# Two decoder layers on one core: GpSimd's shift products of the second pair behind a border, with and without a wait for the inverse root

## The chip, the cores and the metric
The kernel runs on one core of a Trainium2 chip, with TensorE (PE), VectorE (DVE), ScalarE (ACT), GpSimd (POOL) and SyncE (SP), which issues the weight loads. The metric is device time in microseconds of one execution, as the median of several runs.

## The reference, cut to what matters
Two layers of a decoder, 512 tokens, width 1024, float32. Each layer has three sub-layers, each with its own norm, and each norm is modulated by a shift and a scale worked out from a conditioning vector:

```python
h = modulate(rmsnorm(x, norm_ffn1[l]), sh1, sc1)
x = x + 0.5 * g1[:, None, :] * swiglu(h, ffn1_w_up[l], ffn1_w_down[l])
h = modulate(rmsnorm(x, norm_mix[l]), sh2, sc2)
x = x + g2[:, None, :] * hybrid_mixer(h, ...)
h = modulate(rmsnorm(x, norm_ffn2[l]), sh3, sc3)
x = x + 0.5 * g3[:, None, :] * swiglu(h, ffn2_w_up[l], ffn2_w_down[l])
```

with `rmsnorm(x) = x * rsqrt(mean(x*x) + eps) * gain` and `modulate(h) = h * (1 + scale) + shift`. `swiglu` multiplies by a 1024 x 5632 matrix, takes silu(gate) * up, and multiplies by a 2816 x 1024 matrix. So a product of weights with a normalised input is W(x * gain * (1 + scale)) * r + W shift, where r, the inverse root, is one number for each token, and W shift is one number for each output column.

## The kernel before, in words
Activations lie transposed: 128 features of a tile on the partitions, the 512 tokens along the row, 8 tiles `XV[:, k, :]`. Every product is done in three matmuls (`product`, L1598 to L1602): weights and activations are each split in a high part that is rounded (`hi`) and the rest (`lo`), and hi*hi, hi*lo and lo*hi are summed in a PSUM bank. A **unit** is one 128-column tile of weights against all 512 tokens, 8 times 3 matmuls (11 times 3 in the down projection). Units come in **pairs** `b`, unit `s=0` and `s=1`, and so do the buffers `raw[s]`, `Whi[s]`, `Wlo[s]`. SP loads `raw[s]` (L365), ACT makes `Whi` (L568), DVE makes `Wlo` (L943), PE consumes both (L1600 to L1602). ACT's split of a unit waits until PE is through with the unit before it in the same buffer.

The **borders** are the places where one sub-layer ends and the norm of the next begins. PE would be idle there until the sum of squares, its inverse root and the normalised tiles are made. So the first two pairs behind a border are computed from x * gain without the root (`scaled_hi` L614, `scaled_lo` L1010), and afterwards multiplied by the root and given the shift's contribution W shift. In front of the feed-forward borders this is done for the first pair (p=0) and the second pair (p=1); the third pair reads properly normalised tiles. The kernel has three such borders with a second pair: before ffn2 of layer 0, before ffn1 of layer 1, and before ffn2 of layer 1. The two borders before the mixer have a first pair only.

What W shift takes: GpSimd's `shift_products` (L473) multiplies the raw weights of a unit by the shift (L489, 1024 elements a partition), folds them in two halvings (L494, 512 and then 256 elements a partition) and a last one (L497, 128 elements). That is four instructions for a unit, eight for a pair. PE turns the result into a column (`shift_sums`, L1632) and DVE copies that (L1031). For every pair, SP may load the next weights into `raw[s]` only when GpSimd has read it (`shift_read`). GpSimd also adds the squares (`add_squares`, L471) that ACT makes (L579).

The order at such a border, each engine's queue being in program order:
- GpSimd: the adds of squares; shift products of pair p=0, unit 0, then (in between, or behind it before ffn1) the last add of squares, unit 1; then pair p=1, both units. Before the products of p=1 it waits for `rstd_ready`, which DVE's inverse root raises (L477 to L479).
- PE: unit 0 of the first pair (`first_pair`, L1635). After its tile k=2 it does the sum of squares (`sum_squares`, L1593); in unit 1, after tile k=2 (`SPREAD_AT`), it waits for the inverse root and spreads it over the partitions (`spread_rstd`, L1659). Then the shift sums of p=0, two units of the second pair (into the banks `ps_mid`), then the third pair, tile by tile as `split_lo` says that a normalised tile is there.
- DVE: `rstd_of` (L978), a chain of 12 instructions on 4 numbers a partition, each waiting for the one before: L984 (reads PSUM), L985, L986, then three times L990, L991, L992. Behind it, in `first_pairs` (L1033), come the split of a unit of weights, the first normalised tile (`tile`, L1017, which waits for PE's spread), `lo` (L1025), the copies of shift columns, the gates (L1041, L1047, L1049), with more tiles and weight splits in between, up to `lo(7)`.
- ACT: weight splits (L568), the high parts of normalised tiles (L625), silu of the gate (L641), in `first_pairs` (L633).

The call for the second pair is, before ffn2 and before ffn1 of the next layer:

```python
shift_products(l, "ffn2", pair_no(l, FFN2), 1, mod_done, fold_no(l, MIX_FOLD) + 2)
...
shift_products(l + 1, "ffn1", pair_no(l + 1, 0), 1, mod_done, fold_no(l, NEXT_FOLD) + 2)
```

Of the kernel before, what the change touches and what calls it, by code (L numbers as in the profile page):

```python
# [111 lines left out]
def decoder(nc, x, c, positions, norm_ffn1, norm_mix, norm_ffn2, final_norm, w_ada, b_ada,  # L112
# [5 lines left out]
    with ctx:  # L118
# [3 lines left out]
        def sem(name):  # L122
            return ctx.enter_context(nc.semaphore(name))
# [98 lines left out]
        sq_ready, sq_used, ss_ready, rstd_ready, rb_ready = sem("sq_ready"), sem("sq_used"), sem("ss_ready"), sem("rstd_ready"), sem("rb_ready")  # L222
# [17 lines left out]
        carrier = {"sp": sem("sp_carrier"), "pool": sem("pool_carrier"), "dve": sem("dve_carrier")}  # L240
# [38 lines left out]
        def pair_no(l, off):  # L279
            return l * LAYER_PAIRS + off  # L280
# [8 lines left out]
        def fold_no(l, n):  # L289
            return FOLDS * l + n  # L290
# [5 lines left out]
        NORM_NO = {"ffn1": 0, "mix": 1, "ret": 2, "ffn2": 3}  # L296
# [12 lines left out]
        def shift_no(l, name):  # L309
            return LAYER_SHIFTS * l + SHIFT_NO[name]  # L310
# [25 lines left out]
        def angles(eng, st, col, n, ang, tmp):  # L336

            def op(out, in0, *a):
                st.mark(eng.tensor_scalar(out, in0, *a))
                st.wait()  # L340

            op(ang, pos_f[:, :], K[:, K_COL + col:K_COL + col + 1], None, ALU.mult)
            op(n, ang, 1.0 / TWO_PI, ROUND, ALU.mult, ALU.add)
            op(n, n, ROUND, None, ALU.subtract)
            for part in (C1, C2, C3):
                op(tmp, n, part, None, ALU.mult)
                st.mark(eng.tensor_tensor(ang, ang, tmp, ALU.subtract))
                st.wait()
            return eng.tensor_scalar(ang, ang, float(np.float32(-3.1415925)), float(np.float32(3.1415925)), ALU.max, ALU.min)
# [102 lines left out]
        @block.gpsimd  # L452
        def _(pool):
            st = Steps(pool, pool_step)
            pool.wait_ge(const_in, 16 * 2)
            pool.wait_ge(vec_in, 16 * (5 + DEPTH))
            pool.tensor_copy(pos_f[:, :], pos_i[:, :]).then_inc(pos_done, 1)
            pool.wait_ge(pos_done, 1)
            pool.wait_ge(unit_done, 2 * HALF + 3)
            angle_tmp = pos_i[:, :].bitcast(F)  # L460
            angles(pool, st, 0, cos_r[:, :], sin_r[:, :], angle_tmp).then_inc(ang_done_r, 1)
            pool.wait_ge(ang_done_r, 1)
            angles(pool, st, 2, cos_s[:, :], sin_s[:, :], angle_tmp).then_inc(ang_done_s, 1)

            def add_squares(no, k):

                pool.wait_ge(sq_ready, KT * no + k + 1)
                if k > 1:
                    pool.wait_ge(sq_used, ADDED * no + k - 1)
                pool.sem_inc(carrier["pool"], 1)  # L470
                pool.tensor_tensor(square_sum, square_sum, squares[:, k % 2, :], ALU.add).then_inc(sq_used, 1)  # L471

            def shift_products(l, name, b, p, ready, value, between=lambda: None):  # L473

                pool.wait_ge(ready, value)
                pool.sem_inc(carrier["pool"], 1)
                if p:  # L477
                    pool.wait_ge(rstd_ready, 4 * l + NORM_NO[name] + 1)
                    pool.sem_inc(carrier["pool"], 1)  # L479
                for s in range(2):  # L480
                    if s:
                        between()
                    no, acc = shift_no(l, name) + 2 * p + s, shift_acc[2 * p + s]
                    if not isinstance(no, int) or no > 0:
                        pool.wait_ge(shift_made, no)
                    pool.wait_ge(landed[s], 16 * (b + p + 1))
                    pool.sem_inc(carrier["pool"], 1)
                    shift = mod[:, MOD_COL[name]:MOD_COL[name] + KT].unsqueeze(2).broadcast_to([P, KT, P])
                    pool.tensor_tensor(shift_tmp.rearrange("p (k c) -> p k c", c=P), raw[s][:, 0:UP_UNIT].rearrange("p (k c) -> p k c", c=P),  # L489
                                       shift, ALU.mult).then_inc(shift_read, 1)  # L490
                    pool.wait_ge(shift_read, no + 1)
                    pool.sem_inc(carrier["pool"], 1)
                    for n in (UP_UNIT // 2, UP_UNIT // 4):
                        st.mark(pool.tensor_tensor(shift_tmp[:, 0:n], shift_tmp[:, 0:n], shift_tmp[:, n:2 * n], ALU.add))  # L494
                        st.wait()
                        pool.sem_inc(carrier["pool"], 1)
                    pool.tensor_tensor(acc, shift_tmp[:, 0:P], shift_tmp[:, P:2 * P], ALU.add).then_inc(shift_made, 1)  # L497

            with st.loop(0, DEPTH, LAYER_SHIFTS * 2) as l:
                for k in range(1, ADDED):  # L500
                    add_squares(3 * l + 1, k)
                shift_products(l, "mix", pair_no(l, KV_PAIR), 0, mod_done, fold_no(l, MIX_FOLD) + 2,
                               lambda: add_squares(3 * l + 1, ADDED))

                pool.wait_ge(ss_ready, 3 * l + 2)
                pool.sem_inc(carrier["pool"], 1)
                pool.memset(k_all[:, :, 0:P], 0.0).then_inc(k_zero, 1)
                pool.wait_ge(k_zero, l + 1)
                pool.wait_ge(v_done, 2 * TT * (l + 1))
                pool.wait_ge(sv_done, l + 1)  # L510
                pool.wait_ge(k_done, l + 1)
                pool.sem_inc(carrier["pool"], 1)
                def sum_pairs(i):

                    pool.wait_ge(ysq, 2 * (RH * l + i) + 2)
                    pool.sem_inc(carrier["pool"], 1)
                    pool.tensor_tensor(probs[1][:, 0:T], probs[1][:, 0:T], probs[1][:, T:2 * T], ALU.add).then_inc(ysum, 1)

                for i in range(RH):
                    if i % 2 == 0:  # L520

                        pool.wait_ge(unit_done, 2 * pair_no(l, HEAD0) + 6 * i + 2)
                        pool.sem_inc(carrier["pool"], 1)
                        pool.tensor_copy(k_cur, k_all[:, i // 2, :]).then_inc(key_in, 2)

                    pool.wait_ge(y_ps, RH * l + i + 1)
                    pool.sem_inc(carrier["pool"], 1)
                    if i % 2:
                        pool.tensor_copy(v_cur, V[:, i]).then_inc(head_in, 1)
                    else:  # L530
                        pool.tensor_copy(v_cur, V[:, i])
                        pool.wait_ge(o_ps, 2 * (RH * l + i))
                        pool.sem_inc(carrier["pool"], 1)
                        pool.tensor_copy(sv_cur, sv_all[:, i // 2]).then_inc(head_in, 1)
                    if i:
                        sum_pairs(i - 1)
                sum_pairs(RH - 1)
                for k in range(1, ADDED):
                    add_squares(3 * l + 2, k)
                shift_products(l, "ffn2", pair_no(l, FFN2), 0, mod_done, fold_no(l, MIX_FOLD) + 2,  # L540
                               lambda: add_squares(3 * l + 2, ADDED))
                shift_products(l, "ffn2", pair_no(l, FFN2), 1, mod_done, fold_no(l, MIX_FOLD) + 2)
                for k in range(1, ADDED):
                    add_squares(3 * l + 3, k)
                with pool.If(l < DEPTH - 1):
                    shift_products(l + 1, "ffn1", pair_no(l + 1, 0), 0, mod_done, fold_no(l, NEXT_FOLD) + 2)
                add_squares(3 * l + 3, ADDED)
                with pool.If(l < DEPTH - 1):
                    shift_products(l + 1, "ffn1", pair_no(l + 1, 0), 1, mod_done, fold_no(l, NEXT_FOLD) + 2)
# [1437 lines left out]
```

## Time and profile before
| | us |
|---|---|
| median of 3 runs | 2506.55 (2506.16 to 2508.14) |
| the profiled execution | 2506.7 |
| its span, first to last instruction | 2504.9 |
| PE busy | 2472.0 (99%) |
| DVE busy | 1501.5 (60%) |
| ACT busy | 872.2 (35%) |
| GpSimd busy | 210.3 (8%) |

The profile lists busy time by engine over one execution. Times of rows are microseconds from the start of the span. A row of the timeline has its start, its duration, the engine, the line of the kernel, the operation, what it writes and reads, and in brackets the idle time of the engine before it with what ended it. A duration counts from when the engine took the instruction up, so that a time in which it could not get at its data lies inside the duration.

### The profile page before, as it was taken

To read this page: it belongs to the slowest core of one execution; us is meant where nothing else is said; L and a number is where in the kernel's file an instruction comes from. 1 tells how busy PE (TensorE), PEld (TensorE's weight loads), DVE (VectorE), ACT (ScalarE), POOL (GpSimd) and SP (SyncE) were. 2 spreads that over 40 slices of the span, in tenths; PEclk is the share of its full clock that TensorE was granted. 3 is DMA by queue.
4 is the path that set the end of the run, shared out by engine and by line. 5 is a ranking of instruction groups with operands and counts; after the bars stand their busy time and mean duration, and the time that the engine had idled before them with its cause. 6 is when DMAs were issued, how large, how long until landed. Compare 5 with 4: busy or idle time off the path is not lost.

```text
span 2504.9 us, 35621 instructions
## 1 busy us (share of the span) xinstructions
PE 2472.0 (99%) x11468; PEld 2012.8 (80%) x11468; DVE 1501.5 (60%) x2297; ACT 872.2 (35%) x1326; POOL 210.3 (8%) x151
## 2 busy tenths in 40 slices
PE   7999999999999999999999999999999999999998
PEld 5888888877788878888878888887777888788887
DVE  5677778677643477533467677877775435633332
ACT  3222333555423343222332223345553323331332
POOL 0013002000000040000140000210100002200001
PEclk9999999999999999999999999999999999999999
DMA  6665664222134336433336656532222343333332
GB/s 246 195 188 173 187 181 148 86 66 59 53 92 133 94 91 196 140 101 100 102 97 198 186 174 197 165 116 78 59 59 65 95 134 93 88 106 88 96 105 80
DMA packets 488916, 307.31 MB, mean 123 GB/s; under 512 B 9000, under 2 KB 480376, under 8 KB 488184
## 3 DMA queue, kind: packets, MB, share of 16 engines
q1 hardware_dynamic: 420816, 238.73, 32.2%
q10 hardware_dynamic: 68008, 67.48, 8.5%
q8 instruction: 41, 0.67, 0.1%
q14 instruction: 51, 0.42, 0.1%
HBM read 299.89 MB, written 6.29 MB: 122 GB/s over the span
## 4 chain that ended last, share of the span: by engine, by line
PE 94%; DVE 2%; issue 1%; ACT 1%; DMA 0%; DVEq 0%; SPq 0%; ACTq 0%
PE ps_proj L1600 28%; PE ps_proj L1602 28%; PE ps_proj L1601 28%; PE ps_mid L1870 1%; PE ps_mid L1766 1%; PE ps_o L1787 1%; PE ps_mid L1817 1%; PE ps_mid L1819 1%; PE ps_mid L1818 1%; PE ps_mid L1774 1%; PE ps_mid L1862 1%; DMA sb_scratch<-in_x 0%; DVE sb_scratch L1017 0%; PE ps_small L1593 0%; ACT sb_w_hi L568 0%
## 5 line engine op out<-in xcount | busy, mean ns | idle before, releaser
L1600 PE MATMUL ps_proj<-sb_a_hi,sb_w_hi 128*128 128x512 f32 x1908 | 745.5, 391 | 2.2 <-ACT sb_scratch L681 1.7
L1602 PE MATMUL ps_proj<-sb_a_hi,sb_w_lo 128*128 128x512 f32 x1908 | 742.8, 389 | 0.0
L1601 PE MATMUL ps_proj<-sb_a_lo,sb_w_hi 128*128 128x512 f32 x1908 | 742.8, 389 | 0.0
L568 ACT ACTIVATE sb_w_hi<-sb_raw 128x1024 fp32r<-128x1024 f32 (+1 forms) x388 | 430.9, 1110 | 849.1 <-PE ps_proj L1602 816.2
L943 DVE TENSOR_TENSOR sb_w_lo<-sb_raw,sb_w_hi 128x1024 fp32r<-128x1024 f32 (+1 forms) x388 | 514.1, 1325 | 323.2 <-ACT sb_w_hi L568 315.4
L1600 PE MATMUL ps_proj<-sb_h_hi,sb_w_hi 128*128 128x512 f32 x1212 | 480.1, 396 | 6.0 <-DVE sb_h_lo L1025 3.9
L1602 PE MATMUL ps_proj<-sb_h_hi,sb_w_lo 128*128 128x512 f32 x1212 | 472.4, 390 | 0.0
L1601 PE MATMUL ps_proj<-sb_h_lo,sb_w_hi 128*128 128x512 f32 x1212 | 472.2, 390 | 0.0
L1600 PEld LDWEIGHTS ps_proj<-sb_a_hi,sb_w_hi 128*128 128x128 f32 x1908 | 358.5, 188 | 78.7 <-ACT sb_scratch L681 3.0
L1602 PEld LDWEIGHTS ps_proj<-sb_a_hi,sb_w_lo 128*128 128x128 f32 x1908 | 358.4, 188 | 74.6
L1601 PEld LDWEIGHTS ps_proj<-sb_a_lo,sb_w_hi 128*128 128x128 f32 x1908 | 358.6, 188 | 74.3 <-issue 0.5
L1600 PEld LDWEIGHTS ps_proj<-sb_h_hi,sb_w_hi 128*128 128x128 f32 x1212 | 227.6, 188 | 66.4 <-issue 14.0
L1602 PEld LDWEIGHTS ps_proj<-sb_h_hi,sb_w_lo 128*128 128x128 f32 x1212 | 227.6, 188 | 48.5
L1601 PEld LDWEIGHTS ps_proj<-sb_h_lo,sb_w_hi 128*128 128x128 f32 x1212 | 227.7, 188 | 45.3
L955 DVE SCALAR_TENSOR_TENSOR sb_scratch<-sb_scratch,sb_c_act 128x256 f32<-128x256 f32 x448 | 223.7, 499 | 16.1
L471 POOL TENSOR_TENSOR sb_scratch<-sb_scratch 128x512 f32<-128x512 f32 x36 | 61.3, 1702 | 1567.1 <-ACT sb_scratch L579 1567.1
L1097 DVE SCALAR_TENSOR_TENSOR sb_x_or_values<-ps_proj,sb_half_gate,sb_x_or_values 128x512 f32 (+1 forms) x80 | 60.0, 750 | 198.5 <-PE ps_proj L1602 196.9
L1121 DVE TENSOR_TENSOR sb_scratch<-sb_scratch,ps_proj 128x512 f32<-128x512 f32 x82 | 56.4, 688 | 173.7 <-PE ps_proj L1602 173.5
L681 ACT ACTIVATE sb_scratch<-ps_proj 128x512 f32<-128x512 f32 x82 | 49.0, 598 | 303.8 <-PE ps_proj L1602 303.8
L752 ACT ACTIVATE sb_scratch<-sb_scratch,sb_small 128x256 f32<-128x256 f32 x128 | 63.1, 495 | 0.0
L1010 DVE SCALAR_TENSOR_TENSOR sb_h_lo<-sb_x_or_values,sb_gain,sb_h_hi (+1 forms) x40 | 58.7, 1467 | 5.6 <-ACT sb_h_hi L614 5.0
L1124 DVE TENSOR_TENSOR sb_a_lo<-sb_scratch,sb_a_hi 128x512 f32 (+1 forms) x82 | 56.1, 684 | 0.0
(210 smaller groups left out, 1824.6 us busy)
## 6 DMA issues: line engine op xcount, KB each, us to landing
sb_raw<-in_ffn_w_up SPq DMA_DIRECT2D x176, 512.0 KB, 3.8
sb_scratch<-in_w_ada ACTq DMA_DIRECT2D x128, 512.0 KB, 4.2
sb_raw<-in_w_in SPq DMA_DIRECT2D x100, 512.0 KB, 3.8
sb_raw<-in_ffn_w_down SPq DMA_DIRECT2D x64, 704.0 KB, 4.5
sb_raw<-in_w_branch_swa SPq DMA_DIRECT2D x16, 512.0 KB, 3.6
sb_raw<-in_w_branch_ret SPq DMA_DIRECT2D x16, 512.0 KB, 3.6
sb_raw<-in_w_out SPq DMA_DIRECT2D x16, 512.0 KB, 3.5
sb_scratch<-in_w_ada SPq DMA_DIRECT2D x10, 512.0 KB, 7.4
```

What stands on the lines that cost most here:

```text
L471: pool.tensor_tensor(square_sum, square_sum, squares[:, k % 2, :], ALU.add).then_inc(sq_used, 1)
L568: act.activation(Whi[s][:, 0:n], raw[s][:, 0:n], ACT.Copy).then_inc(hi_ready, 1)
L752: last = act.activation(p, p, ACT.Exp, bias=neg_m[w][:, n:n + 1], scale=HD ** -0.5, accum_out=row_sum[w][:, n:n + 1])
L943: dve.tensor_tensor(Wlo[s][:, 0:n], raw[s][:, 0:n], Whi[s][:, 0:n].bitcast(F), ALU.subtract).then_inc(lo_ready, 1)
L955: ins = dve.scalar_tensor_tensor(ada_acc, ada_raw[s][:, k % 4, :], col, ada_acc, ALU.mult, ALU.add)
L1010: dve.scalar_tensor_tensor(Hlo[:, k, :], XV[:, k, :], gain[:, bass.ds(k, 1)], Hhi[:, k, :].bitcast(F), ALU.mult, ALU.subtract).then_inc(gx ...
L1097: dve.scalar_tensor_tensor(XV[:, m, :], pA[s][:, :], half_gate[:, bass.ds(m, 1)], XV[:, m, :], ALU.mult, ALU.add).then_inc(bank_free[s], 1)
L1121: dve.tensor_tensor(work, side, pA[1][:, :], ALU.mult).then_inc(bank_free[1], 1)
L1124: dve.tensor_tensor(Alo[:, i, :], work, Ahi[:, i, :].bitcast(F), ALU.subtract).then_inc(act_lo, 1)
L1600: pe.matmul(bank, Whi[s][:, w], hi, start=first, stop=False)
L1601: pe.matmul(bank, Whi[s][:, w], lo, start=False, stop=False)
L1602: return pe.matmul(bank, Wlo[s][:, w], hi, start=False, stop=last)
```

## The change
GpSimd no longer waits for `rstd_ready` before the shift products of the second pair (p=1). The wait and the increment of a semaphore behind it are taken out; nothing else is touched. The loads that it needs (`landed[s]`), the shift itself (`mod_done`) and its own buffers (`shift_made`, `shift_read`) are waited for as before.

```diff
@@ -474,9 +474,6 @@
 
                 pool.wait_ge(ready, value)
                 pool.sem_inc(carrier["pool"], 1)
-                if p:
-                    pool.wait_ge(rstd_ready, 4 * l + NORM_NO[name] + 1)
-                    pool.sem_inc(carrier["pool"], 1)
                 for s in range(2):
                     if s:
                         between()
```

## Rows read from the trace of the kernel before

**Rows 1.** The page: busy time of each engine, share of the span, instructions.
```profile
PE 2472.0 (99%) x11468; PEld 2012.8 (80%) x11468; DVE 1501.5 (60%) x2297; ACT 872.2 (35%) x1326; POOL 210.3 (8%) x151
```

**Rows 2.** Who waited for whom, PE, whole span: us in total, times, longest.
```profile
PE ps_proj L1600 <- DVE sb_h_lo L1025: 3.9, 8, 0.8
```

**Rows 3.** Instructions of L489: what GpSimd sat idle for before them: us, times.
```profile
  DVE sb_small L992: 10.8, 3
```

**Rows 4.** Timeline of GpSimd, first border: start, duration, what; idle before.
```profile
904.24 0.97 POOL L494 TENSOR_TENSOR sb_scratch<-sb_scratch 128x256 f32<-128x256 f32 x1 [0.18 <-POOL sb_scratch L494]
905.39 0.46 POOL L497 TENSOR_TENSOR sb_scratch<-sb_scratch 128x128 f32<-128x128 f32 x1 [0.18 <-POOL sb_scratch L494]
907.80 1.90 POOL L489 TENSOR_TENSOR sb_scratch<-sb_raw,sb_mod 128x1024 f32<-128x1024 f32 x1 [1.96 <-DVE sb_small L992]
...
912.11 0.73 POOL L494 TENSOR_TENSOR sb_scratch<-sb_scratch 128x256 f32<-128x256 f32 x1 [0.18 <-POOL sb_scratch L494]
```

**Rows 5.** Timeline of DVE, first border: the inverse root.
```profile
904.72 0.52 DVE L985 TENSOR_SCALAR sb_small<-sb_small 128x4 int32<-128x4 int32 x1
905.27 0.17 DVE L986 TENSOR_SCALAR sb_small<-sb_small 128x4 int32<-128x4 int32 x1
905.48 0.39 DVE L990 TENSOR_TENSOR sb_small<-sb_small 128x4 f32<-128x4 f32 x1
...
906.09 0.17 DVE L992 SCALAR_TENSOR_TENSOR sb_small<-sb_small 128x4 f32<-128x4 f32 x1
...
907.28 0.16 DVE L992 SCALAR_TENSOR_TENSOR sb_small<-sb_small 128x4 f32<-128x4 f32 x1
```

**Rows 6.** Timelines of PE, ACT and DVE, first border: spread, third pair's splits, last wait.
```profile
908.94 1.05 PE L1659 MATMUL ps_o<-sb_consts,sb_small 128*128 128x128 f32 x8
...
931.57 0.50 PE L1600 MATMUL ps_proj<-sb_h_hi,sb_w_hi 128*128 128x512 f32 x1 [0.83 <-DVE sb_h_lo L1025]
...
920.12 1.04 ACT L568 ACTIVATE sb_w_hi<-sb_raw 128x1024 fp32r<-128x1024 f32 x1
...
921.20 1.23 DVE L943 TENSOR_TENSOR sb_w_lo<-sb_raw,sb_w_hi 128x1024 fp32r<-128x1024 f32 x1 [0.21 <-ACT sb_w_hi L568]
```

**Rows 7.** Timeline of GpSimd, second border (before ffn1 of layer 1).
```profile
1263.81 1.28 POOL L494 TENSOR_TENSOR sb_scratch<-sb_scratch 128x512 f32<-128x512 f32 x1 [0.18 <-POOL sb_scratch L489]
...
1266.59 1.27 POOL L471 TENSOR_TENSOR sb_scratch<-sb_scratch 128x512 f32<-128x512 f32 x1
1274.75 1.90 POOL L489 TENSOR_TENSOR sb_scratch<-sb_raw,sb_mod 128x1024 f32<-128x1024 f32 x1 [6.89 <-DVE sb_small L992]
```

**Rows 8.** Timeline of DVE, second border: last split and product, start and end of the root.
```profile
1267.10 1.84 DVE L943 TENSOR_TENSOR sb_w_lo<-sb_raw,sb_w_hi 128x1024 fp32r<-128x1024 f32 x1 [0.34 <-ACT sb_w_hi L568]
1268.87 0.74 DVE L1010 SCALAR_TENSOR_TENSOR sb_h_lo<-sb_x_or_values,sb_gain,sb_h_hi 128x512 fp32r<-128x512 f32 x1
1271.97 0.16 DVE L984 TENSOR_SCALAR sb_small<-ps_small 128x4 f32<-128x4 f32 x1 [2.36 <-PE ps_small L1593]
...
1274.15 0.16 DVE L992 SCALAR_TENSOR_TENSOR sb_small<-sb_small 128x4 f32<-128x4 f32 x1
```

**Rows 9.** Timelines of PE and ACT, second border: spread, split for the third pair.
```profile
1277.36 1.05 PE L1659 MATMUL ps_o<-sb_consts,sb_small 128*128 128x128 f32 x8
...
1287.82 1.06 ACT L568 ACTIVATE sb_w_hi<-sb_raw 128x1024 fp32r<-128x1024 f32 x1 [0.15 <-PE ps_mid L1602]
```

**Rows 10.** The page's DMA issues (the last number is us to landing), and SP's timeline.
```profile
sb_raw<-in_ffn_w_up SPq DMA_DIRECT2D x176, 512.0 KB, 3.8
...
903.21 0.37 SPq L365 DMA_DIRECT2D sb_raw<-in_ffn_w_up  x1
...
1269.32 0.37 SPq L365 DMA_DIRECT2D sb_raw<-in_ffn_w_up  x1
```

**Rows 11.** Timeline of DVE, border before the mixer of layer 0: the same pattern.
```profile
414.02 0.51 DVE L985 TENSOR_SCALAR sb_small<-sb_small 128x4 int32<-128x4 int32 x1
...
414.77 0.39 DVE L990 TENSOR_TENSOR sb_small<-sb_small 128x4 f32<-128x4 f32 x1
```

## The prediction
> **What bounds the kernel now.** I read the page first: PE is busy for 2472.0 us of a 2504.9 us span, every other engine far less [rows 1]. So a change pays only through what it does to PE's few waits, and costs only where it makes a new one. The list of waits has one of PE's that lies behind these borders: 3.9 us in 8 places, all for `lo` (L1025), the normalised tiles of the third pair [rows 2]. The view of L489 shows what is removed: GpSimd sat idle 10.8 us in three places for L992, the end of the inverse root [rows 3]: 1.96 us at the first border [rows 4], 6.89 us at the second [rows 7], and the rest, 1.95 us, at the third, whose timeline repeats the first within 0.1 us. Nobody waits at once for what GpSimd makes there: the sums of the second pair's shift are read by PE behind the first unit of the third pair. So GpSimd's idleness costs nothing by itself, and what counts is what its work does to DVE while both run.
>
> **What GpSimd does to DVE.** In the first border GpSimd's L494 runs 904.24 to 905.21 and L497 905.39 to 905.85 [rows 4]. DVE's L985, on four numbers, takes 0.52 us from 904.72 and ends at 905.24, just behind L494; L986 gets through in 0.17 us; L990 takes 0.39 us from 905.48 and ends at 905.87, just behind L497 [rows 5]. Undisturbed, a step takes some 0.17 us (L986, L992), and the chain makes one every 0.20 us: twelve from 1271.97 to 1274.31 at the second border [rows 8]. The same pair of 0.51 and 0.39 us stands at the mixer's border [rows 11]. So a step of the root that meets a running product of GpSimd stands still until that product ends, and then two steps pass (the one that stood, and the one behind it, before GpSimd has started its next 0.18 us later) for each GpSimd instruction. The split of weights, 1.23 us alone [rows 6], takes 1.84 us when L471 is running at its start [rows 7, 8].
>
> The Trainium skill, SBUF — State Buffer, section "Who interferes with whom", has this as a rule: a VectorE instruction with two SBUF inputs, or in a two-port mode, and a GpSimd instruction that reads SBUF exclude each other for a whole instruction, by order of issue. It speaks against this change. The trace agrees (0.52 and 0.39 us for steps of 0.17 us); by the rule the sum is the loss below, and without such a lock it would be the small gain of the second rival.
>
> **The change, part by part.** Removed: a wait and a semaphore increment, three times, neither on PE's path. No instruction, DMA or byte is added. Moved: eight GpSimd instructions a border start 1.9 us earlier (first, third) and some 6 us earlier (second), so that they meet the root's chain, which they followed before. Free durations: L489 1.90, L494 1.28 and 0.73, L497 0.46 us [rows 4, 7]. Is something else late? At the first border the second load left SP at 903.21 and takes 3.8 us to land, 907.0 [rows 10]; it is wanted at 911. The first load of the pair left earlier still. At the second border the second left at 1269.32, there at 1273.1, wanted at 1274.1. So the loads hold nothing back.
>
> First border, step by step. L497 ends at 905.85; GpSimd starts L489 0.20 us later (its gap between two instructions is 0.18, and there are semaphores between), 906.05, and ends it at 907.95. L992 at 906.09 [rows 5] meets it, and ends at 907.98; L990 passes, to 908.17. L494 runs 908.13 to 909.42: L991 ends 909.45, L992 passes. L494 (256) runs to 910.34: L990 ends 910.37, L991 passes. L497 runs 910.52 to 910.98: the last L992 ends at 911.01. Before it ended at 907.44. The root is 3.6 us later. PE began its spread at 908.94 without waiting [rows 6]; its weights need the root, so it now begins about 0.28 us behind it (an estimate, for waking up and loading the weights), at 911.3: PE stands 2.35 us. Not all of this stays. PE later waited 1.4 us there for `lo` (a third of rows 2, with 0.83 us at 931.57 the last), which came from DVE's row of work from 921.20 on, and this began when ACT's split of 920.12 was done [rows 6]. That split waits for PE's unit 0 of the second pair. At the second border ACT started it 10.46 us behind the spread, right when PE released it (1277.36 to 1287.82, [rows 9]); at the first border that would have been 908.94 + 10.46 = 919.40, so ACT, held by its gate (L641), was 0.72 us later than PE allowed. Of the 2.35 us, ACT takes up 0.72, and split, DVE's row and the last tile come 1.6 us later; PE, 2.35 us late, waits the less for them, and ends 1.6 us later. What lies between, in DVE's queue: the split of the second pair's unit 0 starts at 911.04 ahead of GpSimd's second L489 and ends by 912.3; the tiles follow from 912.4, 1.7 us later than before; from there on only four of GpSimd's eight instructions are left to disturb it instead of seven, and I find DVE at its copy of the shift columns 0.3 us later than before. That is hidden, since the next split comes by PE and ACT. So 1.6 us. The third border is the same: 1.6 us.
>
> Second border. GpSimd's L471 ends at 1267.86, L489 can be next, and DVE's split, held until then, runs to 1268.94 [rows 7, 8]. Then L489 to about 1270.65, L1010 behind it to 1271.2 instead of 1269.6 (PE needs that tile after four more tiles behind its sum of squares, at 1274.5: hidden). L494 ends 1272.35; L984 starts at 1271.97 as before, as it reads PSUM. L985 ends 1272.39, L986 passes; L494 (256) to 1273.27 with L990 behind, L991 passes; L497 to 1273.91, L992 behind it, L990 passes; the second unit's L489 to 1276.01, L991, L992; L494 to 1277.48, L990, L991; L494 to 1278.40, the last L992 at 1278.43. Before: 1274.31. PE's spread moves from 1277.36 to 1278.7: 1.35 us. Here ACT's split was released by PE itself [rows 9], so nothing takes this up: 1.35 us.
>
> Sum: 1.6 + 1.35 + 1.6 = 4.55 us on the profiled execution's 2506.7, which lies 0.15 us above the median of the runs; on the median, 2506.55 + 4.55 = 2511.1. Its own range: if GpSimd starts L489 0.1 us later, L992 passes ahead of it and the root ends at 910.66, which makes 1.3 us of 1.6 (sum 3.9); if ACT's slack of 0.72 us isn't there for the taking, 2.35 us of 1.6 (sum 6.1). So 3.9 to 6.1.
>
> **The rivals.**
> *The chain isn't held, and DVE gains.* GpSimd's work ends earlier, and DVE loses less to it behind the root. The most that DVE can use is the 0.72 us by which ACT's split lay behind PE, at the first and third border; at the second PE's own pace holds it. Gain 2 x 0.7 = 1.4 us, 2505.1. For it: DVE did lose there. Against it: two steps of four that met a product were held in rows 5. The same place holds "it doesn't do what it says", something else keeping GpSimd back: 2506.6, against which the load times stand.
> *Held in part.* The root is late, but takes fewer turns with GpSimd than I count, or PE's spread starts sooner: 1 to 3.5 us, about 2509.
> *One step for a product instead of two* (GpSimd's next gets in ahead). First border: seven steps from L992 on, held to 907.95, 909.4, 910.3, 911.0, then by the second unit's 913.1, 914.5, 915.4: PE stands 6.8 us, less 0.7, twice; second border: until about 1280, 2.9 us. Sum 15, 2521.6. It decides as soon as the gap of 0.18 us is too short for a step; L986 in rows 5 did get through it, and this speaks against.
>
> **How the numbers follow.** Forecast 0.72 (3.9 to 6.1 us more, 2510.4 to 2512.7), no hold or no effect 0.10, in part 0.08, one step for each 0.10 with all between 6.1 and 15. The range 2507.5 to 2514.0 leaves out the first rival and most of the last. 0.2% of the time is 5.0 us, about what a measurement of this kernel tells from no change; my forecast lies just inside it. Slower by over 0.2%: some 0.28 of the forecast's 0.72, and the last rival: 0.38. Faster by over 0.2% would need more than all the waits in rows 2: 0.02. Within: 0.60.
>
> **What would show it.** In the new profile L489 of the second pair has no idle time before it for L992; the 12 steps of the root span 6 to 6.5 us (before 2.9 and 2.3), in pairs of a long and a short one; L1659 has PE idle some 2.3, 1.3 and 2.3 us ahead of it, by L992; PE's wait for `lo` shrinks at the first and third border from 1.4 to about 0.7 us and stays 1.0 us at the second; everything behind a border is shifted evenly. I am wrong if PE isn't idle ahead of L1659, or if `lo` comes later by more than 2.4 us at a border.

## The result, and the profile after

The changed kernel takes 2510.94 us (median of 22 runs; the kernel before, beside it, 2506.90 us): 4.0 us more, a ratio of 1.0015 with a 95% interval of 1.0009 to 1.0021. The forecast was 2511.1 us, the likeliest case's own range 2510.4 to 2512.7, the stated range 2507.5 to 2514.0. A second set of runs gave 1.0014 (1.0005 to 1.0023).

Removing three lines moves all line numbers behind them down by three: L489 is now L486, L494 is L491, L497 is L494, L943 is L940, L985 to L992 are L982 to L989, L1593 is L1590, L1659 is L1656.

The page's busy times, against [rows 1]: DVE has 4.5 us more for the same instructions, PE the same.

```profile
PE 2471.9 (99%) x11468; PEld 2012.9 (80%) x11468; DVE 1506.0 (60%) x2297; ACT 872.8 (35%) x1326; POOL 208.0 (8%) x151
```

Whom PE waited for, against [rows 2] (us in total, times, longest):

```profile
PE ps_o L1656 <- DVE sb_small L989: 4.5, 3, 1.6
...
PE ps_proj L1597 <- DVE sb_h_lo L1022: 3.0, 6, 0.8
```

The first row is new: at each of the three borders PE now stands ahead of its spread (L1656) for the end of the inverse root (L989), 4.5 us in all. The second row is what is left of [rows 2], 3.0 instead of 3.9 us: PE comes later and waits less for the normalised tiles.

What ended GpSimd's idle time before its first product, against [rows 3]: DVE isn't among it any more.

```profile
  POOL sb_scratch L494: 1.3, 6
```

The timeline of GpSimd at the first border, against [rows 4]:

```profile
905.02 0.46 POOL L494 TENSOR_TENSOR sb_scratch<-sb_scratch 128x128 f32<-128x128 f32 x1 [0.18 <-POOL sb_scratch L491]
905.74 1.92 POOL L486 TENSOR_TENSOR sb_scratch<-sb_raw,sb_mod 128x1024 f32<-128x1024 f32 x1 [0.26 <-POOL sb_scratch L494]
907.83 1.28 POOL L491 TENSOR_TENSOR sb_scratch<-sb_scratch 128x512 f32<-128x512 f32 x1 [0.18 <-POOL sb_scratch L486]
909.29 0.72 POOL L491 TENSOR_TENSOR sb_scratch<-sb_scratch 128x256 f32<-128x256 f32 x1 [0.18 <-POOL sb_scratch L491]
```

And DVE's at the same place, against [rows 5]:

```profile
905.73 0.17 DVE L989 SCALAR_TENSOR_TENSOR sb_small<-sb_small 128x4 f32<-128x4 f32 x1
905.93 1.75 DVE L987 TENSOR_TENSOR sb_small<-sb_small 128x4 f32<-128x4 f32 x1
907.71 0.16 DVE L988 SCALAR_TENSOR_TENSOR sb_small<-sb_small 128x4 f32<-128x4 f32 x1
907.90 1.23 DVE L989 SCALAR_TENSOR_TENSOR sb_small<-sb_small 128x4 f32<-128x4 f32 x1
909.17 0.16 DVE L987 TENSOR_TENSOR sb_small<-sb_small 128x4 f32<-128x4 f32 x1
909.36 0.67 DVE L988 SCALAR_TENSOR_TENSOR sb_small<-sb_small 128x4 f32<-128x4 f32 x1
910.07 0.16 DVE L989 SCALAR_TENSOR_TENSOR sb_small<-sb_small 128x4 f32<-128x4 f32 x1
```

Read the two together: L987 stands from 905.93 to 907.68, and GpSimd's product ends at 907.66; L989 from 907.90 to 909.13, the fold at 909.11; L988 from 909.36 to 910.03, the next fold at 910.01. Between them a step of 0.16 us passes each time. That is the pattern of [rows 5] continued through the rest of the chain: one long step, one short, for each GpSimd instruction.

PE, ACT and DVE at the first border of the changed kernel, against [rows 6]; 901.30 is the start of the sum of squares, 939.77 the end of PE's wait for ACT in the third pair:

```profile
901.30 1.84 PE L1590 MATMUL ps_small<-sb_consts,sb_scratch 128*128 128x1 f32 x16
...
910.28 1.16 PE L1656 MATMUL ps_o<-sb_consts,sb_small 128*128 128x128 f32 x8 [1.55 <-DVE sb_small L989]
...
932.31 0.50 PE L1597 MATMUL ps_proj<-sb_h_hi,sb_w_hi 128*128 128x512 f32 x1 [0.83 <-DVE sb_h_lo L1022]
...
939.77 0.50 PE L1597 MATMUL ps_proj<-sb_a_hi,sb_w_hi 128*128 128x512 f32 x1 [0.55 <-ACT sb_scratch L678]
...
920.85 1.06 ACT L565 ACTIVATE sb_w_hi<-sb_raw 128x1024 fp32r<-128x1024 f32 x1 [0.80 <-PE ps_mid L1599]
...
921.94 1.23 DVE L940 TENSOR_TENSOR sb_w_lo<-sb_raw,sb_w_hi 128x1024 fp32r<-128x1024 f32 x1 [1.33 <-ACT sb_w_hi L565]
```

The same two ends in the kernel before:

```profile
901.67 1.84 PE L1593 MATMUL ps_small<-sb_consts,sb_scratch 128*128 128x1 f32 x16
...
939.02 0.50 PE L1600 MATMUL ps_proj<-sb_a_hi,sb_w_hi 128*128 128x512 f32 x1 [0.57 <-ACT sb_scratch L681]
```

I call the time between these two the length of a border. It is a good ruler: over the twelve profiles of this study the same code at a border gave the same length within 0.05 us (one exception, told below), while the median of a kernel moved by up to 0.7 us from one set of runs to another. The first border was 37.35 us and is 38.47 us; the third 37.35 and 38.45; the second 36.66 and 38.28. Together 1.12 + 1.62 + 1.10 = 3.84 us more. The profiled spans differ by 3.0 us (2507.9 and 2504.9); the missing 0.84 us lies outside the borders: 0.37 us before the first one, 0.41 us between the first and the second (0.40 of it in the idle time that the view of waits puts down to issue, 1.94 us before and 1.54 after, at a branch of PE's program), 0.03 us in each of the two other stretches. The issue gap lay between 1.44 and 1.94 us over all profiles, and differed by 0.33 us between the two profiles of one kernel (psum_wait, 1.44 and 1.77), so I don't put it down to the change.

The second border, where the first product starts in front of DVE's L1007 and runs until 1271.44 (GpSimd, DVE, PE, ACT):

```profile
1268.57 2.87 POOL L486 TENSOR_TENSOR sb_scratch<-sb_raw,sb_mod 128x1024 f32<-128x1024 f32 x1
...
1267.84 1.85 DVE L940 TENSOR_TENSOR sb_w_lo<-sb_raw,sb_w_hi 128x1024 fp32r<-128x1024 f32 x1 [0.34 <-ACT sb_w_hi L565]
1269.62 2.38 DVE L1007 SCALAR_TENSOR_TENSOR sb_h_lo<-sb_x_or_values,sb_gain,sb_h_hi 128x512 fp32r<-128x512 f32 x1
1272.31 0.16 DVE L981 TENSOR_SCALAR sb_small<-ps_small 128x4 f32<-128x4 f32 x1 [0.31 <-PE ps_small L1590]
...
1278.50 0.67 DVE L989 SCALAR_TENSOR_TENSOR sb_small<-sb_small 128x4 f32<-128x4 f32 x1
...
1270.43 1.84 PE L1590 MATMUL ps_small<-sb_consts,sb_scratch 128*128 128x1 f32 x16
...
1279.22 1.16 PE L1656 MATMUL ps_o<-sb_consts,sb_small 128*128 128x128 f32 x8 [1.35 <-DVE sb_small L989]
...
1289.78 1.06 ACT L565 ACTIVATE sb_w_hi<-sb_raw 128x1024 fp32r<-128x1024 f32 x1 [2.10 <-PE ps_mid L1599]
```

The product takes 2.87 us where a free one takes 1.90: it was taken up while DVE's split (until 1269.69) was running. So the holding goes both ways. L1007, taken up behind the product's start, takes 2.38 us for 0.74, and the root's 12 steps, from 1272.31 to 1279.17, take 6.86 us for 2.34.

### The profile page after: what moved, and what is told of

Read it like the earlier page. It is cut to its first block, busy times and chain, and to the rows that moved or that the text cites. A ratio compares the mean times of both kernels' runs of the same rounds, so it can differ in the third digit from the quotient of the medians.

```text
span 2507.9 us, 35617 instructions
## 1 busy us (share of the span) xinstructions
PE 2471.9 (99%) x11468; PEld 2012.9 (80%) x11468; DVE 1506.0 (60%) x2297; ACT 872.8 (35%) x1326; POOL 208.0 (8%) x151
## 4 chain that ended last, share of the span: by engine, by line
PE 94%; DVE 3%; issue 1%; ACT 1%; DMA 0%; DVEq 0%; SPq 0%; ACTq 0%
PE ps_proj L1597 28%; PE ps_proj L1599 27%; PE ps_proj L1598 27%; PE ps_mid L1867 1%; PE ps_mid L1763 1%; PE ps_o L1784 1%; PE ps_mid L1814 1%; PE ps_mid L1815 1%; PE ps_mid L1816 1%; PE ps_mid L1771 1%; PE ps_mid L1859 1%; DMA sb_scratch<-in_x 0%; ACT sb_w_hi L565 0%; DVE sb_scratch L1014 0%; DVE sb_h_lo L1022 0%
## 5 line engine op out<-in xcount | busy, mean ns | idle before, releaser
L940 DVE TENSOR_TENSOR sb_w_lo<-sb_raw,sb_w_hi 128x1024 fp32r<-128x1024 f32 (+1 forms) x388 | 508.7, 1311 | 323.7 <-ACT sb_w_hi L565 316.0
L1007 DVE SCALAR_TENSOR_TENSOR sb_h_lo<-sb_x_or_values,sb_gain,sb_h_hi (+1 forms) x40 | 60.3, 1508 | 5.6 <-ACT sb_h_hi L611 5.2
```

The lines of the kernel that those rows point to most:

```text
L940: dve.tensor_tensor(Wlo[s][:, 0:n], raw[s][:, 0:n], Whi[s][:, 0:n].bitcast(F), ALU.subtract).then_inc(lo_ready, 1)
L1007: dve.scalar_tensor_tensor(Hlo[:, k, :], XV[:, k, :], gain[:, bass.ds(k, 1)], Hhi[:, k, :].bitcast(F), ALU.mult, ALU.subtract).then_inc(gx ...
```

## The experiments

All of them start from the kernel before ("with the wait") or from the changed kernel ("without"). The table has the three border lengths from the profile, their sum against the 111.36 us of the kernel before, when the root ended at the first border (from the start of the sum of squares), and the timed ratio. Line numbers in the rows of an experiment are those of its own kernel.

| kernel | borders, us | sum | root ends | ratio (95%) |
|---|---|---|---|---|
| before | 37.35, 36.66, 37.35 | 0 | 5.77 | 1 |
| changed | 38.47, 38.28, 38.45 | +3.84 | 8.93 | 1.0015 (1.0009 to 1.0021) |
| only_ffn2 | 38.47, 36.64, 38.45 | +2.20 | 8.92 | 1.0013 (1.0004 to 1.0022) |
| only_ffn1 | 37.36, 38.26, 37.37 | +1.63 | 5.76 | 1.0006 (0.9997 to 1.0015) |
| psum_nowait | 37.26, 36.63, 37.27 | -0.20 | 5.17 | 0.9992 (0.9983 to 1.0001) |
| psum_wait | 36.76, 36.64, 36.76 | -1.20 | 5.17 | 0.9988 (0.9979 to 0.9997) |
| spread4_nowait | 37.60, 36.82, 37.60 | +0.66 | 8.95 | 1.0004 (0.9995 to 1.0013) |
| memset_nowait | 36.66, 36.64, 36.65 | -1.41 | 5.76 | 0.9992 (0.9983 to 1.0001) |
| split4_nowait | 37.78, 37.18, 37.80 | +1.40 | 8.25 | 1.0010 (1.0001 to 1.0019) |
| split4_gaps | 36.65, 36.66, 36.64 | -1.41 | 6.68 | 0.9990 (0.9981 to 0.9999) |
| psum_wait_again | 36.76, 36.65, 36.75 | -1.20 | 5.17 | 0.9991 (0.9981 to 1.0000) |
| after_again | 38.48, 38.11, 38.47 | +3.70 | 8.95 | 1.0014 (1.0005 to 1.0023) |

The intervals of the ratios of the ten experiments are about 0.09% wide on either side, 2.3 us. So the sums, of 0.2 to 3.8 us, are read from the borders, and the ratios say whether they agree. They do: each sum lies within the interval of its ratio. But they don't tell experiments that are 1 us apart from one another; such a difference rests on one or two profiles of each kernel.

**One border at a time** (only_ffn2 and only_ffn1).

```diff
-                if p:
+                if p and name == "ffn1":        # only_ffn2: the wait is gone before ffn2
-                if p:
+                if p and name == "ffn2":        # only_ffn1: the wait is gone before ffn1
```

> The wait is taken out at the two borders before ffn2 and kept at the one before ffn1. Theory (the steps of the inverse root are held by GpSimd's products, PE stands ahead of its spread): from PE's sum of squares to the end of its wait for ACT's gate in the third pair, the first and third border take 1.1 us more than before, the second none; 2.2 us more in all, about 2509.1 us. Rival (the early products pay or cost across borders, by loads or by buffers handed on): the sum doesn't split by border, this kernel is near before or near the full loss of 4.0 us.

> The wait is taken out at the border before ffn1 of layer 1 alone. Theory: the second border takes 1.6 us more than before, the others none, about 2508.5 us, and with the kernel that frees the other two borders the losses add up to the full one (1.6 + 2.2 against 4.0). Rival (the loss is made at the borders before ffn2, where GpSimd starts earlier by less but in the middle of the root): no loss here, 2506.9 us.

Measured: +1.12, -0.02 and +1.10 us in the one, +0.01, +1.60 and +0.02 us in the other. Their sum is the changed kernel's 3.84 us within 0.01. The sizes were known from the changed kernel's profile before these two ran; open was whether they would part by border, and they do. The loss is made at each border by itself, at that border's own wait.

**The root out of GpSimd's way** (psum_nowait and psum_wait). The running value y is kept in PSUM; each step then reads at most one operand from SBUF. Only the last step writes y to SBUF, where PE reads it. The number of steps stays 12.

```diff
+                final = y
+                if psum:
+                    y = pS[:, 64:64 + n]
...
+                    to = final if turn == 2 else y
...
-                        lambda: dve.tensor_tensor(a, y, y, ALU.mult),
-                        lambda: dve.scalar_tensor_tensor(a, a, -0.5, v, ALU.mult, ALU.mult),
-                        lambda: dve.scalar_tensor_tensor(y, a, 1.5, y, ALU.add, ALU.mult),
+                        lambda: dve.scalar_tensor_tensor(a, v, -0.5, y, ALU.mult, ALU.mult),
+                        lambda: dve.tensor_tensor(a, a, y, ALU.mult),
+                        lambda to=to: dve.scalar_tensor_tensor(to, a, 1.5, y, ALU.add, ALU.mult),
```

> No wait, and the running value of the root lies in PSUM, so that no step of the chain reads two operands from SBUF (12 steps as before, v*y and then *y in place of y*y and then *v). Theory (steps are held since they want two SBUF inputs while GpSimd reads): the chain makes its 12 steps in about 2.4 us with GpSimd running, PE has no wait ahead of the spread, and DVE gains what ACT's slack of 0.7 us allows at the first and third border: about 1.4 us less than the kernel before, some 2505.5 us. Rival 1 (GpSimd's early work costs by itself, by its semaphores or the loads that it releases): the loss of 4 us stays. Rival 2 (the chain is held by anything that GpSimd does): steps of 1.2 to 1.9 us stay.

> The wait is kept, and the running value of the root lies in PSUM, as in the other kernel of this kind: the control for it. Theory: the steps that the first pair's last two GpSimd instructions hold at the first and third border (0.35 and 0.22 us) run free, the root ends 0.6 us earlier there, GpSimd's second pair starts as much earlier, and PE gains 0 to 0.3 us a border: within 1 us of the kernel before, 2506.0 to 2506.9 us. So the kernel without the wait and with PSUM is faster than this one by what GpSimd's early end is worth, 0.5 to 1.4 us. Rival (the wait is worth something to DVE beyond the chain): this kernel is faster than the one without the wait by 1 us or more.

In psum_nowait GpSimd's instructions run through the whole of the root, with gaps of 0.18 and 0.26 us, and yet no step of the root is held (first the timeline of GpSimd, then DVE's; L991, L992 and L996 are the three steps of a turn, L985 is the second step of the chain):

```profile
905.65 1.90 POOL L486 TENSOR_TENSOR sb_scratch<-sb_raw,sb_mod 128x1024 f32<-128x1024 f32 x1 [0.26 <-POOL sb_scratch L494]
907.72 1.28 POOL L491 TENSOR_TENSOR sb_scratch<-sb_scratch 128x512 f32<-128x512 f32 x1 [0.18 <-POOL sb_scratch L486]
...
904.26 0.17 DVE L985 TENSOR_SCALAR ps_small<-sb_small 128x4 int32<-128x4 int32 x1
...
905.83 0.16 DVE L991 SCALAR_TENSOR_TENSOR sb_small<-sb_small,ps_small 128x4 f32<-128x4 f32 x1
906.02 0.16 DVE L992 TENSOR_TENSOR sb_small<-sb_small,ps_small 128x4 f32<-128x4 f32 x1
906.22 0.16 DVE L996 SCALAR_TENSOR_TENSOR sb_small<-sb_small,ps_small 128x4 f32<-128x4 f32 x1
907.73 2.35 DVE L940 TENSOR_TENSOR sb_w_lo<-sb_raw,sb_w_hi 128x1024 fp32r<-128x1024 f32 x1 [1.36 <-ACT sb_w_hi L565]
```

PE has no wait at the spread, and the loss of 3.84 us is gone. So the second rival falls (steps of 1.2 to 1.9 us didn't stay), and so does the first as it was put (the loss of 4 us didn't stay). But the gain of 1.4 us that I expected on top didn't come: 0.20 us instead. Here the control tells: with the wait kept, the same root gives 1.20 us. Its theory had said at most 0.3 us a border, and it was 0.59 at the first and third; the expectation was missed. The rival of the control (the wait is worth something to DVE beyond the chain) asked for 1 us or more between the two, and got 1.00, 0.50 at each of those two borders and nothing at the second. So with the root out of the way GpSimd's early work does cost something by itself, behind the root. DVE's split is taken up at 907.73, 0.01 us behind GpSimd's fold (907.72), and takes 2.35 us for 1.23. With the wait kept, GpSimd's products come 1.1 us later against PE; the split then stands only through the last 0.9 us of the first product, and takes 1.98 us:

```profile
907.27 1.98 DVE L943 TENSOR_TENSOR sb_w_lo<-sb_raw,sb_w_hi 128x1024 fp32r<-128x1024 f32 x1 [1.36 <-ACT sb_w_hi L568]
```

At the first border, summed up from the root's end to DVE's copy of the shift columns and against the free durations of memset_nowait, DVE was held 4.6 us in the kernel before, 4.6 us in psum_nowait and 4.1 us in psum_wait: GpSimd's earlier end bought DVE nothing.

**PE's need moved back** (spread4_nowait).

```diff
-                unit(b, g, 1, h_tile, used=used, after={SPREAD_AT: spread})
+                unit(b, g, 1, h_tile, used=used, after={SPREAD_AT if between else 4: spread})
```

> No wait, and PE spreads the root after tile k=4 of the unit instead of k=2 (at the borders before the feed-forward parts), 1.37 us later in its own work. Theory (the loss is PE's standing at the spread, and only a little of it DVE's lateness behind): PE stands 0.3 us or less ahead of the spread instead of 1.35 to 1.6, the root ends as late as without the wait, and of the loss of 3.8 us at the three borders some 3 us are given back, about 2507.7 us. Rival (DVE's row behind the root sets the end of the border, PE's wait is only where it shows): the wait moves to the normalised tiles (L1022), and the loss stays 4 us.

The root ends as late as without the wait (8.95 us), and PE stands 0.2 us:

```profile
909.49 1.16 PE L1656 MATMUL ps_o<-sb_consts,sb_small 128*128 128x128 f32 x8 [0.21 <-DVE sb_small L989]
...
928.82 0.50 PE L1597 MATMUL ps_proj<-sb_h_hi,sb_w_hi 128*128 128x512 f32 x1 [0.36 <-DVE sb_h_lo L1022]
...
930.62 0.50 PE L1597 MATMUL ps_proj<-sb_h_hi,sb_w_hi 128*128 128x512 f32 x1 [0.84 <-DVE sb_h_lo L1022]
```

3.2 of the 3.84 us are given back (expected: some 3), and the wait did not move to the tiles: 1.20 us there, 0.2 more than in the changed kernel and less than before. The root's lateness cost almost only through the place where PE asked for it; 0.66 us stay.

**GpSimd that reads nothing** (memset_nowait). Every one of the second pair's GpSimd instructions becomes a memset of the same output, so the kernel leaves out the second pair's shift.

```diff
+                    if p:
+                        pool.memset(shift_tmp, 0.0).then_inc(shift_read, 1)
+                    else:
...
+                        if p:
+                            st.mark(pool.memset(shift_tmp[:, 0:n], 0.0))
+                        else:
...
+                    if p:
+                        pool.memset(acc, 0.0).then_inc(shift_made, 1)
+                    else:
...
```

> No wait, and the second pair's eight GpSimd instructions only write (memsets of the same outputs) and read nothing, so the shift of the second pair is left out of the result. Theory (a GpSimd instruction holds a step only while it reads SBUF): steps of the chain behind the first pair's last product take 0.2 us each, PE doesn't wait ahead of the spread, DVE's later work is free of holds too: 1.4 us less than the kernel before at most, about 2505.5 us. Rival (any GpSimd instruction holds a step): steps are still held for the length of a memset, and PE still stands at the spread.

GpSimd's memset of 1024 elements, and DVE's steps inside it (L996 to L998 are the three steps of a turn):

```profile
906.98 0.96 POOL L487 MEMSET sb_scratch<- 128x1024 f32 x1 [0.24 <-POOL sb_scratch L503]
...
907.19 0.16 DVE L996 TENSOR_TENSOR sb_small<-sb_small 128x4 f32<-128x4 f32 x1
907.39 0.16 DVE L997 SCALAR_TENSOR_TENSOR sb_small<-sb_small 128x4 f32<-128x4 f32 x1
907.58 0.16 DVE L998 SCALAR_TENSOR_TENSOR sb_small<-sb_small 128x4 f32<-128x4 f32 x1
```

Three steps pass inside one instruction of 0.96 us, though each of them takes both its inputs from SBUF. The rival falls: for these steps it takes GpSimd's reading, and not only its running. The Trainium skill, SBUF — State Buffer, section "Who interferes with whom", says just this, that two SBUF inputs on VectorE contend with a GpSimd instruction that reads SBUF and not with one that only writes; 0.16 us here beside 1.75 us in the changed kernel agree with it. With a second pair that reads nothing a border takes 36.65 us, and all three are alike, 1.41 us in all under the kernel before, as expected. These memsets are also shorter than the products (0.96 us for 1.90), so the run alone doesn't part the reading from the length; split4_gaps below, with longer products that do read, gives the same borders. So the 1.41 us are what the second pair's products cost the kernel before, by holding DVE.

**Many short products** (split4_nowait and split4_gaps). The first product of a unit is cut in four of 256 elements; in the second kernel GpSimd also waits for each piece before it starts the next.

```diff
-                    pool.tensor_tensor(...).then_inc(shift_read, 1)
+                    parts = 4 if p else 1
+                    for q in range(parts):
+                        k0, k1 = KT * q // parts, KT * (q + 1) // parts
+                        last = pool.tensor_tensor(...[:, k0:k1, :], ...[:, k0:k1, :], shift[:, k0:k1, :], ALU.mult)
+                        if q < parts - 1:        # split4_gaps only
+                            st.mark(last)
+                            st.wait()
+                    last.then_inc(shift_read, 1)
```

(The arguments are cut to `...`. split4_gaps also raises the count of marks of the loop around it, by 12 a layer, for the waits that it adds.)

> No wait, and the second pair's first product is cut in four instructions of 256 elements a partition each, so that GpSimd's work gets longer (some 3.6 for 1.9 us a unit) but has more gaps. Theory (two steps of the chain pass for each GpSimd instruction, however long it is): at the first border the last six steps pass in three pieces, the root ends about 7.2 us behind the start of the sum of squares instead of 8.9, at the second about 7.0 instead of 8.7, PE stands 0.2 us or less at the spread, and what is left of the loss is DVE's being held behind it: 0 to 2 us more than the kernel before. Rival (the chain loses in proportion to GpSimd's busy time beside it): the root ends later than without the cut, the loss is 5 us or more.

> No wait, the second pair's first product in four pieces as before, and now GpSimd waits for each piece before it starts the next, which makes a gap of about 0.18 us between them (without it the pieces stood back to back, 2.35 us for four, and one step of the root passed for each, 0.54 us apart). Theory (it is the gap behind a GpSimd instruction that lets the second step through): two steps pass for each piece, the root ends 6.7 to 7.0 us behind the start of the sum of squares at the first border instead of 8.25, PE doesn't stand at the spread at any border, and the three borders together cost 0.5 us more than before at most instead of 1.4. Rival (one step for each piece, gap or not, and the gaps only make GpSimd's work longer): the root ends at 8.4 or later.

Without the gaps (GpSimd, then DVE; x4 is the four pieces together):

```profile
907.08 2.35 POOL L489 TENSOR_TENSOR sb_scratch<-sb_raw,sb_mod 128x256 f32<-128x256 f32 x4 [0.26 <-POOL sb_scratch L499]
...
907.77 0.54 DVE L993 SCALAR_TENSOR_TENSOR sb_small<-sb_small 128x4 f32<-128x4 f32 x1
908.34 0.54 DVE L994 SCALAR_TENSOR_TENSOR sb_small<-sb_small 128x4 f32<-128x4 f32 x1
908.92 0.54 DVE L992 TENSOR_TENSOR sb_small<-sb_small 128x4 f32<-128x4 f32 x1
909.49 0.17 DVE L993 SCALAR_TENSOR_TENSOR sb_small<-sb_small 128x4 f32<-128x4 f32 x1
909.69 1.21 DVE L994 SCALAR_TENSOR_TENSOR sb_small<-sb_small 128x4 f32<-128x4 f32 x1
```

With them:

```profile
906.90 2.73 POOL L489 TENSOR_TENSOR sb_scratch<-sb_raw,sb_mod 128x256 f32<-128x256 f32 x4 [0.26 <-POOL sb_scratch L502]
...
907.08 0.47 DVE L995 TENSOR_TENSOR sb_small<-sb_small 128x4 f32<-128x4 f32 x1
907.59 0.16 DVE L996 SCALAR_TENSOR_TENSOR sb_small<-sb_small 128x4 f32<-128x4 f32 x1
907.78 0.46 DVE L997 SCALAR_TENSOR_TENSOR sb_small<-sb_small 128x4 f32<-128x4 f32 x1
908.28 0.16 DVE L995 TENSOR_TENSOR sb_small<-sb_small 128x4 f32<-128x4 f32 x1
908.48 0.47 DVE L996 SCALAR_TENSOR_TENSOR sb_small<-sb_small 128x4 f32<-128x4 f32 x1
908.98 0.16 DVE L997 SCALAR_TENSOR_TENSOR sb_small<-sb_small 128x4 f32<-128x4 f32 x1
```

The first of these missed its expectation: the root ended at 8.25 us and not at 7.2, PE stood 0.88 us, and the loss was 1.40 us. I had counted two steps for each piece; but pieces of one line with no wait between them stand back to back (2.35 us for four), and then one step passes for each, one every 0.57 us. Its rival (proportional to busy time) was wrong too: the root ended earlier than with the product uncut (8.25 us against 8.93), and the loss was less than half. The second was made to tell whether the gap is what lets the second step through, and it does: a long step and a short one in turn, the root at 6.68 us (expected 6.7 to 7.0), no wait at the spread. GpSimd's first product now takes 2.73 us a unit for 1.90, and yet the three borders are 1.41 us shorter than before, the same 36.65 us as with a GpSimd that reads nothing. I had expected up to 0.5 us more than before, so the size of the gain wasn't foreseen. At this place DVE's split takes 1.61 us where it took 2.58 before; summed up as above, DVE was held 1.3 us behind the root.

**The PSUM root with the wait again, beside the changed kernel** (psum_wait_again and after_again; no edit).

> The wait is kept and the root's running value lies in PSUM: the kernel that came out fastest, timed a second time beside the changed kernel. Its three borders took 1.2 us less than before in the trace; so 0.9995 of the time of before, within 0.1% either way, and 5 us (0.2%) less than the changed kernel.

> The changed kernel once more, on the same chip as the two others: the three borders take 3.8 us more than before as in its first trace (38.47, 38.28, 38.45 us from the sum of squares to the end of the gate's wait), 1.0015 of the time of before.

Both came out as expected. split4_gaps has a median of 2504.78 us, psum_wait 2505.59 and 2505.16 us, the kernel before 2507.1 to 2507.5 us beside them. Both are faster than the kernel before by about 0.1% (the intervals end at 0.9999 for the one, 0.9997 and 1.0000 for the other) and than the changed one by about 0.25%; which of the two is the faster the runs don't tell. The one border that didn't repeat within 0.05 us is the second one without the wait, 38.28, 38.26 and 38.11 us: the length goes with the issue gap of PE's branch in front of it, 1.54, 1.56 and 1.72 us in the three, by which GpSimd's first product, which waits for nothing of PE's, lies earlier or later against the root (it ends 1.01, 1.01 and 0.84 us behind the start of the sum of squares). A fourth profile fits: in spread4_nowait, with a gap of 1.66 us, the second border's root ended at 8.65 us, between the 8.73 of 1.56 and the 8.59 of 1.72. No run tried this alone.

## Why the prediction was right

By its own steps:

- **The bound.** A change pays or costs only through PE's waits: the 3.84 us of the borders are PE's, DVE's 4.5 us more of busy time and GpSimd's 10.8 us less of waiting are worth nothing by themselves. Shown: where PE asks for the root later, as late a root costs 0.66 us (spread4_nowait).
- **The steps of the root are held by GpSimd's reads, two pass for each instruction.** Shown by the rows after, by memset_nowait and by the PSUM root. That two pass, and not one, hangs on GpSimd's gap of 0.18 us: split4_nowait and split4_gaps. The last rival (one step for each instruction, 15 us) is real as a mechanism; it decides where GpSimd's instructions stand back to back, which the products here don't. The reason that the forecast gave against it, L986 getting through in the gap of 0.18 us, held.
- **First and third border, 1.6 us each: measured 1.12 and 1.10.** GpSimd started 0.26 us behind its last fold and not 0.20, so one step more passed ahead of it (L989 at 905.73 took 0.17 us, the product was taken up at 905.74). The two starts lie 0.01 us apart; that the order fell this way and not the other the forecast could not have seen. This is the lower end that the prediction gave, with its root later by 3.22 us (measured 8.93 less 5.77, that is 3.16) and a loss of 1.3. The other 0.2 us is PE's waking: I took 0.28 us from the root's end to the spread. No run shows that figure: it was 0.05 us (8.93 and 8.98), as already in the rows of the kernel before where PE waits for DVE's L1025 (0.05 or 0.06 us each). Against it, the spread itself took 1.16 us instead of 1.05. So the spread came 1.71 us later, and ended 1.82 us later.
- **ACT's slack of 0.72 us takes up a part.** 1.82 less 1.10 is 0.72. ACT's split came 1.10 us later (from 18.45 to 19.55 us behind the start of the sum of squares), now released by PE. And the border free of GpSimd is 37.35 less 36.65 = 0.70 us shorter, the same slack from the other side. Shown.
- **Second border, 1.35 us: measured 1.62.** The spread moved from 7.27 to 8.79 us, 1.52, and took 0.11 us longer. I had the first product end at 1270.65; it ended at 1271.44, which is 0.45 us more behind the start of the sum of squares (1.01 us for 0.56), as GpSimd worked 0.4 us later against PE in this execution (the issue gap again); the shorter waking gave 0.23 us back. A term of the sum that was mis-sized, at the place where the sum could least be known.
- **Sum, 4.55 us: measured 3.84 in the borders, 4.0 by the medians.** By the medians inside the case's own range of 3.9 to 6.1, at its lower end; by the borders 0.06 us below it. That the median, 2510.94, lies 0.2 us from the forecast of 2511.1 is partly luck: the kernel before was 2506.90 us beside it and not the 2506.55 that the forecast started from, and the first and third border fell short by 1.0 us together while the second was 0.27 us over.
- **The rival in which the chain isn't held and DVE gains at most 1.4 us** (the first of the list, once called the second). The bound is right: 1.41 us is what memset_nowait and split4_gaps give. But psum_nowait, which is that very case, gave 0.20 us. What failed is the thought that DVE gains because GpSimd ends earlier: it is held by other instructions instead, for as long.

Of the signs named beforehand, the pairs of a long and a short step, the missing idle time of GpSimd and the new wait ahead of the spread came. The wait was 1.55, 1.35 and 1.55 us, where 2.3, 1.3 and 2.3 had been said, and the root's 12 steps spanned 6.07, 6.86 and 6.06 us for 6 to 6.5. PE's wait for the tiles at the first and third border fell to 1.0 us and not to 0.7.

## What to carry to other kernels

A chain of tiny DVE instructions that each wait for the one before suffers badly beside a GpSimd that reads SBUF: here every second step stood until the end of a GpSimd instruction, so a chain of 2.3 us took 6.9 us at the second border, beside products of 0.5 to 1.9 us. Before an idle wait on GpSimd is taken out, ask which DVE instructions it kept apart from GpSimd's, and not what GpSimd gains. If the two must overlap, cut GpSimd's work in short instructions with a wait between them: here that took 1.41 us off the borders of the kernel with the wait, about 0.1% by the timed runs. A chain whose steps read at most one operand from SBUF ran unhindered, but without the wait it only came out even (0.20 us), since GpSimd then held DVE's later work as much as before; its 1.20 us, again about 0.1%, came with the wait kept.

## What the runs showed of the hardware

- GpSimd instructions in a row with no wait between them left room for one held DVE instruction at each boundary (split4_nowait: steps 0.57 us apart beside pieces of 0.59 us); a gap of 0.18 us let a second one of 0.16 us through (the changed kernel, split4_gaps).
- The holding goes both ways: a GpSimd product of 1.90 us, taken up while DVE's split was running, took 2.87 us (the changed kernel, second border).
- A DVE instruction of four elements is held like one of 1024: 1.75 us for 0.16 in the changed kernel, beside a split with 2.35 us for 1.23 in psum_nowait.
- A DVE instruction with one operand in SBUF and one in PSUM ran in 0.16 us beside GpSimd's L486 (psum_nowait). L985, with one operand, ran from SBUF to PSUM in 0.17 us beside its fold L491 of 903.78 to 904.75; from SBUF to SBUF the same operation took 0.52 us in the kernel before. So two operands in SBUF are not the only case that is held.
- A memset on GpSimd (1024 elements a partition, 0.96 us) held none of the root's steps (memset_nowait).
- The granted clock was 0.997 or 0.998 of full speed over each whole span, that is the level of 2.4 GHz; PE's new standing of 1.2 to 1.6 us at the borders did not lower it: the 25 us behind the first such wait (910.28 to 935.28) show 1.00.
